# Cross attention's sample values computed in full fp32, with V standing still under columns of probabilities

## The chip, the cores and the metric

One Trainium2 chip, of which the program uses one core. The metric is the time of one execution on the device in microseconds (us), the median of several. Engines are named as in the profile: PE is TensorE's matmul, PEld its weight load, DVE is VectorE, ACT is ScalarE, POOL is GpSimd, SP is SyncE.

## The reference

One inference step of a two-layer decoder trunk, for a prompt of 256 tokens and for 8 sample sequences of one token each, in fp32. Each layer runs a feed-forward block, a mixer (state space and retention in layer 0, mLSTM in layer 1), cross attention and a second feed-forward block. The part that counts here is cross attention:

```python
def cross_attn(h, k, v, w_q, w_o):
    bsz, l, _ = h.shape
    q = (h @ w_q).reshape(bsz, l, X_HEADS, X_HEAD_DIM)
    s = jnp.einsum('blhd,bmhd->bhlm', q, k.astype(q.dtype)).astype(F32) * (X_HEAD_DIM ** -0.5)
    p = jax.nn.softmax(s, axis=-1).astype(h.dtype)
    o = jnp.einsum('bhlm,bmhd->blhd', p, v.astype(h.dtype)).reshape(bsz, l, D_MODEL)
    return o @ w_o
```

There are 4 heads of 256 dimensions over 256 memory tokens. The prompt's K and V are computed from `mem_prompt` by a linear layer (`w_xkv`) and are outputs too. Each of the 8 samples has K and V of its own, read from `cache_mem_k` and `cache_mem_v`: 256 x 1024 fp32 numbers, 1 MB each, for each sample and layer. For a sample, `o` is one row of probabilities for each head times that sample's V.

## The kernel before

The kernel is a list of stages. Each stage gives work to some of the five engines, and each engine runs its share of all stages in the order of the list; semaphores tie the engines together. So what stands ahead of a wait in an engine's list is done first, and what stands behind it waits too.

**Linear layers** (class `Linear`, L170) walk over chunks of 256 output columns. SP loads a chunk of weights (`raw`, four slots), ACT rounds it to its upper half (`whi`, L205), DVE subtracts to get the lower half (`wlo`, L211), two chunks ahead of PE. PE then does three products for each tile, upper by upper, upper by lower and lower by upper, so that two halves in the rounded type fp32r replace one fp32 product. A chunk is 2 output tiles x 8 k tiles x 3 products, which is 48 matmuls. A linear layer can have hooks: other stages, whose instructions are put behind the matmuls of chunk l on PE, and next to that chunk's step on the other engines.

**Cross attention** (function `cross`, L1653, run once for each layer) has two such linear layers over the memory: the K linear layer carries the samples' scores in its hooks (`SampleScores`, with `spread`, L708 and L709, which broadcasts a query row to all partitions), the V linear layer (L1873, `turned`, 256 columns, lines L247 to L249) carries the samples' values:

- hook 0: `SampleSoftmax`, and the transposes that bring the prompt's K into token order (`k_turn`);
- hook 1: `SplitV` for samples 0 and 1, `prob_turn` (two transposes that put the samples' probabilities into columns, `pTs`, memory tokens on partitions), `MaskProbs`, then `SampleValues` for samples 0 and 1;
- hooks 2 and 3: `SplitV` and `SampleValues` for samples 2 and 3, and 4 and 5;
- behind the layer: the same for 6 and 7, then `SampleRows`.

`MaskProbs` (L1781) spreads the probabilities over 64 columns with zeros between them, in two halves (`pmh`, `pml`), so that all samples can add into the same 8 rows of PSUM. `SplitV` (L1801) makes two halves of a sample's V: ACT writes `vh` (L1814), DVE writes `vl` over the loaded values (L1820). `SampleValues` (L1823) then needs, for each sample, 2 halves of the memory x 4 heads x 3 products = 24 matmuls (L1845 to L1847). The stationary operand is 128 x 8 (masked probabilities), and 256 columns of V stream. Each ends in rows (8 samples x 1024), which `SampleRows` copies out (L1853) and `SampleOut` transposes back into columns (L1860) while the prompt's scores run.

The loads of V go through POOL's queue in pieces of half a sample (`load_v`, L1684, 512 KB). `vc` holds two samples. The first four pieces are issued by `FirstV`, well ahead. Every later one waits until the matmuls on the piece two samples before it have ended (L1831), since `vl` is stored in place. `SampleValues`' loads are followed on POOL by the stores of the prompt's K and V (`Keep`, L1878).

Behind the stage come `Scores` (L1892, the prompt's scores; L1896 waits for all sample values), `SampleOut`, the transposes of the prompt's probabilities, `Values` (L1929, products at L1938), and the output projection.

In the profile, a matmul on fp32 operands shows as two records and one on fp32r as one: L2271 is 64 matmuls in the program and 128 records.

Of the kernel before, what the change touches and what calls it, by code (L numbers as in the profile page):

```python
# [14 lines left out]
F32 = mybir.dt.float32  # L15
F32R = mybir.dt.float32r
ALU = mybir.AluOpType
# [3 lines left out]
P = 128  # L21
D = 1024
KD = D // P
NP = 256
# [17 lines left out]
def build(nc, A, O):  # L42
    with ExitStack() as ctx:
# [755 lines left out]
        def mixer_ab():  # L799
# [819 lines left out]
            class RReady(Stage):  # L1619
                def pe(S, e):  # L1620
# [5 lines left out]
        X = {n: sem_of("x_" + n) for n in ("mem_in", "score", "nmax", "exp", "prob", "pv", "oh", "ol", "qb", "kused", "smax", "sexp", "sprob",  # L1626
                                           "spv", "soh", "sol", "qh", "ql", "vh", "vl", "pm", "pmh", "pml", "ost", "spo")}
        KR = 8
# [4 lines left out]
        def cross_buffers():  # L1633
# [9 lines left out]
                qtl=place("qtl", [NS, 2, 512], F32R, at=R + 82176), qth=place("qth", [NS, 2, 512], F32R, at=R + 88064),  # L1643
                ost=place("ost", [NS, 2, 512], at=R + 88064),
                vh=place("vh", [P, 2, 2, D], F32R, at=R + 65792), vl=place("vl", [P, 2, 2, D], F32R, at=R),
                pm=place("pm", [P, 8, 64], at=R + 92160), pml=place("pml", [P, 8, 64], F32R, at=R + 92160),
                pmh=place("pmh", [P, 8, 64], F32R, at=R + 94208),  sc=place("sc", [P, 2, 32], at=R + 86272),
                ps_=place("ps_", [32, MEM], at=R + 86528), pTs=place("pTs", [P, 64], at=R + 87552),
                st=place("st", [P, 4, 8], at=R + 87808), sst=place("sst", [32, 4], at=R + 87936),
                kc=[place(f"kc{i}", [P, 4, D], at=R + at) for i, at in enumerate((65792, 40960))],  # L1650
                 vc=place("vc", [P, 2, 2, D], at=R))

        def cross(layer):  # L1653
# [12 lines left out]
            class Load(Stage):  # L1666
# [8 lines left out]
                def dve(S, e):  # L1675
                    for q, n in kept:
                        e.wait_ge(q, n)
# [5 lines left out]

            def load_v(e, u):  # L1684
                e.dma_start(B.vc[:, u // 2 % 2, u % 2, :], A["cache_mem_v"][layer, u // 2, (u % 2) * P:(u % 2 + 1) * P].rearrange("p h d -> p (h d)")).then_inc(vc_in[u % 4], 16)

# [12 lines left out]
            class FirstV(Stage):  # L1699
                def pool(S, e):  # L1700
                    mem_split(e)
                    for u in range(4):
                        load_v(e, u)
            stages.append(FirstV())
# [75 lines left out]
            ps_ready = turned()  # L1780
            class MaskProbs(Stage):  # L1781


                def pool(S, e):
                    if lc:
                        e.wait_ge(X["sol"], lc)
                    e.memset(B.pm[:, :, :], 0.0).then_inc(X["pm"], 1)

                def dve(S, e):
                    ps_ready(e)  # L1790
                    e.wait_ge(X["pm"], 2 * lc + 1)
                    e.tensor_copy(B.pm[:, :, 0:64:9].rearrange("p (m h) b -> p m h b", m=2),
                                  B.pTs[:, :].rearrange("p (m b h) -> p m h b", m=2, b=NS)).then_inc(X["pm"], 1)
                    e.wait_ge(X["pmh"], lc + 1)
                    e.tensor_tensor(B.pml[:, :, :], B.pm[:, :, :], B.pmh[:, :, :].bitcast(F32), ALU.subtract).then_inc(X["pml"], 1)

                def act(S, e):
                    e.wait_ge(X["pm"], 2 * lc + 2)
                    nc.scalar.activation(B.pmh[:, :, :], B.pm[:, :, :], ACT.Copy).then_inc(X["pmh"], 1)

            class SplitV(Stage):  # L1801

                def __init__(S, b):
                    S.b = b

                def act(S, e):
                    b = S.b
                    if b < 2:
                        e.wait_ge(X["kused"], 2 * NS * (lc + 1))
                    for m_ in range(2):  # L1810
                        e.wait_ge(vc_in[2 * (b % 2) + m_], 16 * (4 * lc + b // 2 + 1))
                        if b >= 2:
                            e.wait_ge(X["spv"], 2 * (NS * lc + b - 2) + m_ + 1)
                        nc.scalar.activation(B.vh[:, b % 2, m_, :], B.vc[:, b % 2, m_, :], ACT.Copy).then_inc(X["vh"], 1)  # L1814

                def dve(S, e):
                    b = S.b
                    for m_ in range(2):
                        e.wait_ge(X["vh"], 2 * (NS * lc + b) + m_ + 1)
                        e.tensor_tensor(B.vl[:, b % 2, m_, :], B.vc[:, b % 2, m_, :], B.vh[:, b % 2, m_, :].bitcast(F32),  # L1820
                                        ALU.subtract).then_inc(X["vl"], 1)

            class SampleValues(Stage):  # L1823

                def __init__(S, b):
                    S.b = b

                def pool(S, e):
                    for u in (2 * S.b, 2 * S.b + 1):
                        if u + 4 < 2 * NS:  # L1830
                            e.wait_ge(X["spv"], 2 * NS * lc + u + 1)  # L1831
                            load_v(e, u + 4)

                def pe(S, e):
                    b = S.b
                    if b == 0:
                        e.wait_ge(X["pml"], lc + 1)
                    for m_ in range(2):
                        e.wait_ge(X["vl"], 2 * (NS * lc + b) + m_ + 1)
                        for h in range(XH):  # L1840
                            o = psum[0:NS, 4 + h // 2, (h % 2) * XD:(h % 2 + 1) * XD]
                            ph, pl = B.pmh[:, m_ * XH + h, b * 8:b * 8 + 8], B.pml[:, m_ * XH + h, b * 8:b * 8 + 8]
                            vh, vl = B.vh[:, b % 2, m_, h * XD:(h + 1) * XD], B.vl[:, b % 2, m_, h * XD:(h + 1) * XD]

                            e.matmul(o, ph, vh, start=b == 0 and m_ == 0 and h % 2 == 0, stop=False)  # L1845
                            e.matmul(o, ph, vl, start=False, stop=False)  # L1846
                            m = e.matmul(o, pl, vh, start=False, stop=b == NS - 1 and m_ == 1 and h % 2 == 1)  # L1847
                        m.then_inc(X["spv"], 1)

            class SampleRows(Stage):  # L1850
                def dve(S, e):
                    e.wait_ge(X["spv"], 2 * NS * (lc + 1))
                    e.tensor_copy(B.ost[:, :, :], psum[0:NS, 4:6, :]).then_inc(X["ost"], 1)  # L1853

            class SampleOut(Stage):

                def pe(S, e):
                    e.wait_ge(X["ost"], lc + 1)
                    for t in range(KD):
                        m = e.transpose(psum[:, 5, t * NS:(t + 1) * NS], B.ost[:, t // 4, (t % 4) * P:(t % 4 + 1) * P], ident[0:NS, 0:NS])  # L1860
                    m.then_inc(X["spo"], 1)

                def act(S, e):
                    e.wait_ge(X["spo"], lc + 1)
                    nc.scalar.activation(B.oh[:, :, NP:T], psum[:, 5, 0:64].rearrange("p (t b) -> p t b", t=KD), ACT.Copy).then_inc(X["soh"], 1)

                def dve(S, e):
                    e.wait_ge(X["soh"], lc + 1)
                    e.tensor_tensor(B.ol[:, :, NP:T], psum[:, 5, 0:64].rearrange("p (t b) -> p t b", t=KD), B.oh[:, :, NP:T].bitcast(F32),
                                    ALU.subtract).then_inc(X["sol"], 1)  # L1870

            SV, SP = [SampleValues(b) for b in range(NS)], [SplitV(b) for b in range(NS)]
            Linear(W, 4, KD, 2, by_cols(W, D), (B.mh, B.ml), dve=v_out, cols=256, turned=True, early=True,  # L1873
                   hooks={0: [SampleSoftmax()] + k_turn, 1: SP[0:2] + prob_turn + [MaskProbs()] + SV[0:2],
                          2: SP[2:4] + SV[2:4], 3: SP[4:6] + SV[4:6]})
            kv_out = evicted()
# [8 lines left out]
            stages.append(Keep())  # L1885
            for b in (6, 7):
                stages.extend([SP[b], SV[b]])
            stages.append(SampleRows())
            tot["stores"] += 32
            pending.append((stored["pool"], tot["stores"]))  # L1890

            class Scores(Stage):  # L1892

                def pe(S, e):
                    kv_out(e)
                    e.wait_ge(X["spv"], 2 * NS * (lc + 1))  # L1896
                    for u in range(8):
                        h, lb = u // 2, u % 2
                        if u >= 2:
                            e.wait_ge(X["exp"], 8 * lc + u - 1)  # L1900
                        for d in range(2):
                            m = e.matmul(psum[:, u % 2, 0:MEM], B.xq[:, 2 * h + d, lb * P:(lb + 1) * P], B.Kf[:, 2 * h + d, :], start=d == 0, stop=d == 1)  # L1902
                        m.then_inc(X["score"], 1)
# [519 lines left out]
```

## Time and profile before

| what | us |
|---|---|
| median of 3 runs | 2179.12 |
| lowest and highest | 2172.78, 2183.26 |
| the profiled execution | 2174.99 |
| its span, first to last instruction | 2173.2 |
| mean granted TensorE clock | 0.922 of 2.4 GHz |
| PE busy | 1906.6 (88%) |
| DVE busy | 1375.7 (63%) |
| ACT busy | 896.0 (41%) |

Three views serve here. The busy time by window cuts a stretch into pieces and gives for each how long an engine was busy, the records in it, and the clock that was granted to TensorE (1.00 is 2.4 GHz, 0.50 is 1.2 GHz). The waits say who waited for whom. The timeline lists instructions in order, with equal neighbours merged into one row: its start, its length from the first start to the last end, and the count of records.

### The profile page before, as it was taken

Reading aid. Unit: us, or ns where it says so; the run is one execution under the profiler, and the core shown is the slowest. Engines: PE = TensorE matmul, PEld = TensorE weight load, DVE = VectorE, ACT = ScalarE, POOL = GpSimd, SP = SyncE. Lnnn points to the kernel's source line nnn. Section 1 sums busy time; section 2 is a strip of 40 time slices with the busy share of each in tenths; the row PEclk is TensorE's granted clock in tenths of the full one; section 3 lists DMA queues with packets and bytes.
Section 4 is the critical chain, followed back from the end, with each engine's and each line's share of the span. In section 5 each row is a group of like instructions: output and inputs, shape, how many; then the busy total and the mean of one; then the engine's idle time right before and its main releaser. Section 6 shows DMA issues by size and latency. Waiting matters only on the chain. (4 is left out here: it accounts for less than half of the span.)

```text
span 2173.2 us, 35020 instructions
## 1 busy us (share of the span) xinstructions
PE 1906.6 (88%) x13769; PEld 1744.7 (80%) x13769; DVE 1375.7 (63%) x2352; ACT 896.0 (41%) x1143; POOL 202.1 (9%) x292
## 2 busy tenths in 40 slices
PE   6999886996688768998899999999968698899996
PEld 5999786985355467987779999999956597679996
DVE  4665595698767565448567656665652567557654
ACT  4434344346655445332434334433422532434331
POOL 0001101101111000111110011001001021110011
PEclk9999998899799888998999999999985898999998
DMA  6656852336778424666526656656606266526652
GB/s 179 181 163 188 156 168 65 113 117 189 247 261 298 148 79 114 176 233 232 203 90 182 184 160 191 186 157 195 191 29 163 78 217 229 206 86 174 185 160 82
DMA packets 462782, 361.49 MB, mean 166 GB/s; under 512 B 12297, under 2 KB 435493, under 8 KB 462629
## 3 DMA queue, kind: packets, MB, share of 16 engines
q1 hardware_dynamic: 409056, 254.35, 39.9%
q0 software_dynamic: 20192, 71.95, 10.8%
q10 hardware_dynamic: 33424, 33.70, 4.6%
q8 instruction: 72, 1.18, 0.2%
q14 instruction: 38, 0.31, 0.0%
HBM read 321.49 MB, written 38.66 MB: 166 GB/s over the span
## 5 line engine op out<-in xcount | busy, mean ns | idle before, releaser
L211 DVE TENSOR_TENSOR wlo<-raw,whi 128x2048 fp32r<-128x2048 f32 (+2 forms) x262 | 558.9, 2134 | 268.4 <-ACT whi L205 267.7
L252 PE MATMUL psum<-xnh,whi 128*128 128x264 f32 x2328 | 676.9, 291 | 10.1 <-DVE cols L885 9.8
L253 PE MATMUL psum<-xnl,whi 128*128 128x264 f32 x2328 | 668.7, 287 | 0.0
L254 PE MATMUL psum<-xnh,wlo 128*128 128x264 f32 x2328 | 667.5, 287 | 0.0
L205 ACT ACTIVATE whi<-raw 128x2048 fp32r<-128x2048 f32 (+2 forms) x262 | 463.3, 1770 | 190.7 <-DMA raw<-in_w_ffn_out 76.8
L252 PEld LDWEIGHTS psum<-xnh,whi 128*128 128x128 f32 x2328 | 449.0, 193 | 15.7 <-DVE cols L885 8.6
L253 PEld LDWEIGHTS psum<-xnl,whi 128*128 128x128 f32 x2328 | 448.8, 193 | 1.2
L254 PEld LDWEIGHTS psum<-xnh,wlo 128*128 128x128 f32 x2328 | 445.9, 192 | 0.0
L252 PE MATMUL psum<-Hh,whi 128*128 128x264 f32 x704 | 200.5, 285 | 0.0
L254 PE MATMUL psum<-Hh,wlo 128*128 128x264 f32 x704 | 200.0, 284 | 0.0
L253 PE MATMUL psum<-Hl,whi 128*128 128x264 f32 x704 | 199.1, 283 | 0.0
L722 ACT ACTIVATE sg<-sg 128x264 f32<-128x264 f32 x88 | 37.4, 425 | 288.0 <-DVE sg L726 287.9
L254 PEld LDWEIGHTS psum<-Hh,wlo 128*128 128x128 f32 x704 | 132.6, 188 | 0.0
L253 PEld LDWEIGHTS psum<-Hl,whi 128*128 128x128 f32 x704 | 132.5, 188 | 0.0
L252 PEld LDWEIGHTS psum<-Hh,whi 128*128 128x128 f32 x704 | 132.3, 188 | 0.0
L374 ACT ACTIVATE xnh<-x,g 128x264 fp32r<-128x264 f32 x56 | 27.6, 514 | 154.1 <-DVE x L384 83.8
L459 PE MATMUL psum<-sq,ones 128*128 128x264 f32 (+1 forms) x128 | 46.2, 504 | 43.3 <-ACT sq L445 42.4
L405 POOL TENSOR_TENSOR sq<-x 128x264 f32 (+1 forms) x52 | 39.5, 760 | 416.1 <-DVE x L382 217.1
L726 DVE TENSOR_TENSOR sg<-psum,rstd 128x264 f32<-128x264 f32 x88 | 38.0, 431 | 58.8 <-PE psum L254 58.7
L459 PEld LDWEIGHTS psum<-sq,ones 128*128 128x128 f32 x128 | 25.8, 236 | 58.8 <-issue 39.6
L393 POOL MEMSET acc<- 128x528 f32 x8 | 4.4, 544 | 735.3 <-DVE ht L729 533.0
L729 DVE TENSOR_TENSOR ht<-sg,psum 128x264 f32<-128x264 f32 x88 | 37.8, 430 | 54.4 <-ACT sg L722 54.4
(479 smaller groups left out, 3425.3 us busy)
## 6 DMA issues: line engine op xcount, KB each, us to landing
raw<-in_w_ffn_in SPq DMA_DIRECT2D x176, 512.0 KB, 4.9
raw<-in_w_in_ab SPq DMA_DIRECT2D x88, 512.0 KB, 4.4
raw<-in_w_ffn_out SPq DMA_DIRECT2D x64, 384.0 KB, 4.0
raw<-in_w_ffn_out SPq DMA_DIRECT2D x64, 320.0 KB, 3.3
sb<-in_state_ret POOLq DMA_DIRECT2D x32, 512.0 KB, 5.6
out<-sb ACTq DMA_DIRECT2D x32, 512.0 KB, 4.8
raw<-in_w_out_ab SPq DMA_DIRECT2D x32, 512.0 KB, 4.5
kc<-in_cache_mem_k POOLq DMA_DIRECT2D x32, 512.0 KB, 5.9
```

The costliest lines, as they stand in the source:

```text
L205: nc.scalar.activation(whi[:, c % SLOTS, 0:m], raw[:, c % SLOTS, 0:m], ACT.Copy).then_inc(hi_done, 1)
L211: nc.vector.tensor_tensor(wlo[:, c % SLOTS, 0:m], raw[:, c % SLOTS, 0:m], whi[:, c % SLOTS, 0:m].bitcast(F32), ALU.subtract).then_inc(lo_d ...
L252: e.matmul(out, a, hi[:, kk, 0:S.cols], start=first, stop=False)
L253: e.matmul(out, a, lo[:, kk, 0:S.cols], start=False, stop=False)
L254: m = e.matmul(out, b, hi[:, kk, 0:S.cols], start=False, stop=final)
L374: nc.scalar.activation(xnh[:, t, :], x[:, t, :], ACT.Copy, scale=g1[:, gcol + t:gcol + t + 1]).then_inc(xh_done, 1)
L393: e.memset(acc[:, :, :], 0.0).then_inc(acc_done, 1)
L405: e.tensor_tensor(sq[:, at, :], xs, xs, ALU.mult).then_inc(xs_ready, 1)
L459: e.matmul(psum[:, SSB, 0:S.n], ones[:, :], sq[:, t % 2, 0:S.n], start=t % S.g == 0, stop=t % S.g == S.g - 1).then_inc(ss_done, 1)
L722: nc.scalar.activation(sg[:, par, :], sg[:, par, :], ACT.Silu).then_inc(gate_ready, 1)
L726: e.tensor_tensor(sg[:, par, :], psum[:, 2 * par, 0:T], rstd1[:, 0, :], ALU.mult).then_inc(gate_scaled, 1)
L729: e.tensor_tensor(ht[:, par, :], sg[:, par, :], psum[:, 2 * par + 1, 0:T], ALU.mult).then_inc(bank_free, 1)
```

## The change

The samples' V is no longer split. `SampleValues` takes the loaded fp32 values as the stationary operand, a tile of 128 tokens x 128 dimensions, and streams one column: the probabilities of that sample and head, in fp32. For each sample there are 8 tiles of dimensions x 2 halves of the memory = 16 fp32 matmuls instead of 24 on fp32r, and each writes one column of PSUM, already in the layout that `SampleOut` wants. `MaskProbs`, `SplitV`, `SampleRows` and the 8 transposes of `SampleOut` go. `vc` becomes two tiles of two samples each; the second takes the place of half of the samples' K buffers, so `LaterV` loads samples 2 and 3 once the scores of sample 5 have been computed. Later loads wait for the matmuls of the sample four before, not two.

```diff
-                vh=place("vh", [P, 2, 2, D], F32R, at=R + 65792), vl=place("vl", [P, 2, 2, D], F32R, at=R),
-                 vc=place("vc", [P, 2, 2, D], at=R))
+                vc=[place(f"vc{i}", [P, 2, 2, D], at=R + at) for i, at in enumerate((0, 65792))])
...
-            def load_v(e, u):
-                e.dma_start(B.vc[:, u // 2 % 2, u % 2, :], A["cache_mem_v"][layer, u // 2, (u % 2) * P:(u % 2 + 1) * P].rearrange("p h d -> p (h d)")).then_inc(vc_in[u % 4], 16)
+            def load_v(e, b):
+                for m_ in range(2):
+                    e.dma_start(B.vc[b // 2 % 2][:, b % 2, m_, :],
+                                A["cache_mem_v"][layer, b, m_ * P:(m_ + 1) * P].rearrange("p h d -> p (h d)")).then_inc(vc_in[b % 4], 16)
...
+            class LaterV(Stage):
+                def pool(S, e):
+                    e.wait_ge(X["kused"], 2 * NS * lc + 12)
+                    for b in (2, 3):
+                        load_v(e, b)
...
             class SampleValues(Stage):
                 def pool(S, e):
-                    for u in (2 * S.b, 2 * S.b + 1):
-                        if u + 4 < 2 * NS:
-                            e.wait_ge(X["spv"], 2 * NS * lc + u + 1)
-                            load_v(e, u + 4)
+                    b = S.b
+                    if b + 4 < NS:
+                        e.wait_ge(X["spv"], NS * lc + b + 1)
+                        load_v(e, b + 4)
                 def pe(S, e):
                     b = S.b
                     if b == 0:
-                        e.wait_ge(X["pml"], lc + 1)
-                    for m_ in range(2):
-                        e.wait_ge(X["vl"], 2 * (NS * lc + b) + m_ + 1)
-                        for h in range(XH):
...
-                            e.matmul(o, ph, vh, start=b == 0 and m_ == 0 and h % 2 == 0, stop=False)
-                            e.matmul(o, ph, vl, start=False, stop=False)
-                            m = e.matmul(o, pl, vh, start=False, stop=b == NS - 1 and m_ == 1 and h % 2 == 1)
-                        m.then_inc(X["spv"], 1)
+                        ps_ready(e)
+                    e.wait_ge(vc_in[b % 4], 32 * (2 * lc + b // 4 + 1))
+                    for t in range(KD):
+                        h = t // 2
+                        for m_ in range(2):
+                            i = m_ * 32 + b * XH + h
+                            m = e.matmul(psum[:, 4, t * NS + b:t * NS + b + 1], B.vc[b // 2 % 2][:, b % 2, m_, t * P:(t + 1) * P], B.pTs[:, i:i + 1],
+                                         start=m_ == 0, stop=m_ == 1)
+                    m.then_inc(X["spv"], 1)
...
-            class SampleRows(Stage):
-                def dve(S, e):
-                    e.wait_ge(X["spv"], 2 * NS * (lc + 1))
-                    e.tensor_copy(B.ost[:, :, :], psum[0:NS, 4:6, :]).then_inc(X["ost"], 1)
...
             Linear(W, 4, KD, 2, by_cols(W, D), (B.mh, B.ml), dve=v_out, cols=256, turned=True, early=True,
-                   hooks={0: [SampleSoftmax()] + k_turn, 1: SP[0:2] + prob_turn + [MaskProbs()] + SV[0:2],
-                          2: SP[2:4] + SV[2:4], 3: SP[4:6] + SV[4:6]})
+                   hooks={0: [LaterV(), SampleSoftmax()] + k_turn, 1: prob_turn + SV[0:2], 2: SV[2:4], 3: SV[4:6]})
...
-            for b in (6, 7):
-                stages.extend([SP[b], SV[b]])
-            stages.append(SampleRows())
+            stages.extend(SV[6:8])
```

## Rows read from the trace of the kernel before

**Rows 1.** The page: the span and each engine's busy time.
```profile
span 2173.2 us, 35020 instructions
PE 1906.6 (88%) x13769; PEld 1744.7 (80%) x13769; DVE 1375.7 (63%) x2352; ACT 896.0 (41%) x1143; POOL 202.1 (9%) x292
```

**Rows 2.** Windows, PE alone, layer 0: stretch, length, busy (records), clock, DMA share, GB/s.
```profile
1046.30:1051.10 4.80, 0.31 (x3) 0.71 0.67 217
1051.10:1058.60 7.50, 7.49 (x49) 0.73 0.34 120
1058.60:1064.20 5.60, 5.60 (x50) 1.00 0.67 217
1080.90:1084.40 3.50, 0.00 (x0) 1.00 1.00 365
1084.40:1091.80 7.40, 7.26 (x48) 0.77 0.82 332
```

**Rows 3.** Waits, 1046 to 1092: engine, line, whom for: total, times, longest.
```profile
ACT vh L1814 <- DMA vc<-in_cache_mem_v: 21.4, 12, 5.7
PE psum L1845 <- DVE pml L1795: 4.5, 1, 4.5
PE psum L1845 <- DVE vl L1820: 3.7, 1, 3.7
```

**Rows 4.** Waits, the same stretch of layer 1, 1860 to 1906.
```profile
PE psum L1845 <- DVE pml L1795: 5.3, 1, 5.3
PE psum L1845 <- DVE vl L1820: 3.3, 1, 3.3
```

**Rows 5.** Chain that ended last, layer 1, before the last pair: start, us, what.
```profile
1892.01 4.65 DMA vc<-in_cache_mem_v
```

**Rows 6.** Timeline, ACT and DVE, layer 0: start, us, line, names, shapes, records.
```profile
1020.64 0.42 DVE L1739 CUSTOM_DVE_ANT_0 kc<-kc,psum 128x256 f32<-128x256 f32 x1
1046.64 0.22 ACT L616 ACTIVATE pTs<-psum 128x64 f32<-128x64 f32 x1 [0.19 <-PE psum L598]
```

**Rows 7.** The page's DMA issues: KB of each, us to landing.
```profile
vc<-in_cache_mem_v POOLq DMA_DIRECT2D x32, 512.0 KB, 5.8
```

**Rows 8.** Timeline, PE: a spread behind a K chunk; mLSTM's sample states (`SampleC`).
```profile
1004.85 0.50 PE L708 MATMUL psum<-qth,sel 8*128 8x512 f32 x1
...
1650.40 3.57 PE L2271 MATMUL psum<-cq,ccb 128*128 128x1 f32 x16
```

**Rows 9.** Timeline, PE, mLSTM's prompt states, layer 1.
```profile
1624.46 0.50 PE L2118 MATMUL psum<-ones,cktm 128*128 128x1 f32 x4
1625.77 0.39 PE L2118 MATMUL psum<-ones,cktm 128*128 128x1 f32 x3
```

**Rows 10.** Windows in `SampleC`: PE, PEld, DVE, ACT, POOL busy (records), clock, DMA.
```profile
1645.00:1650.00 5.00, 5.00 (x20) 4.53 (x20) 1.66 (x4) 3.55 (x9) 0.78 (x1) 0.50 0.68 229
```

**Rows 11.** Windows of 1 us, columns as in rows 10: K chunk, spreads, K chunk.
```profile
1006.00:1007.00 1.00, 1.00 (x6) 0.55 (x5) 0.92 (x5) 0.00 (x0) 0.00 (x0) 1.00 0.83 208
1007.00:1008.00 1.00, 1.00 (x7) 1.00 (x8) 1.00 (x7) 0.00 (x0) 0.17 (x1) 0.69 0.98 324
1017.00:1018.00 1.00, 1.00 (x10) 1.00 (x8) 1.00 (x7) 0.00 (x0) 0.00 (x0) 0.81 0.92 275
```

**Rows 12.** Windows of 1 us, columns as in rows 10: around the first pair.
```profile
1048.00:1049.00 1.00, 0.00 (x0) 0.00 (x0) 1.00 (x2) 0.00 (x0) 0.00 (x0) 0.67 1.00 344
1055.00:1056.00 1.00, 1.00 (x10) 0.71 (x9) 0.00 (x0) 0.00 (x0) 0.00 (x0) 0.91 0.58 164
```

**Rows 13.** Windows, PE alone, columns as in rows 2: a K chunk behind spreads.
```profile
1006.90:1014.30 7.40, 7.40 (x50) 0.77 1.00 336
```

**Rows 14.** Timeline, PE, end of the stage in layer 1.
```profile
1906.04 1.97 PE L1902 MATMUL psum<-Kf,xq 128*128 128x256 f32 x8
1915.35 0.66 PE L1860 MATMUL psum<-ident,ost 8*128 8x8 f32 x8
1917.36 1.06 PE L598 MATMUL psum<-ident,pp 128*128 128x128 f32 x8 [1.35 <-issue]
```

More of the change, by code:

```diff
@@ L1626, in build @@
         X = {n: sem_of("x_" + n) for n in ("mem_in", "score", "nmax", "exp", "prob", "pv", "oh", "ol", "qb", "kused", "smax", "sexp", "sprob",
-                                           "spv", "soh", "sol", "qh", "ql", "vh", "vl", "pm", "pmh", "pml", "ost", "spo")}
+                                           "spv", "soh", "sol", "qh", "ql")}
         KR = 8
@@ L1643, in cross_buffers @@
                 qtl=place("qtl", [NS, 2, 512], F32R, at=R + 82176), qth=place("qth", [NS, 2, 512], F32R, at=R + 88064),
-                ost=place("ost", [NS, 2, 512], at=R + 88064),
-                vh=place("vh", [P, 2, 2, D], F32R, at=R + 65792), vl=place("vl", [P, 2, 2, D], F32R, at=R),
-                pm=place("pm", [P, 8, 64], at=R + 92160), pml=place("pml", [P, 8, 64], F32R, at=R + 92160),
-                pmh=place("pmh", [P, 8, 64], F32R, at=R + 94208),  sc=place("sc", [P, 2, 32], at=R + 86272),
+                sc=place("sc", [P, 2, 32], at=R + 86272),
                 ps_=place("ps_", [32, MEM], at=R + 86528), pTs=place("pTs", [P, 64], at=R + 87552),
@@ L1701, in pool @@
                     mem_split(e)
-                    for u in range(4):
-                        load_v(e, u)
+                    for b in range(2):
+                        load_v(e, b)
             stages.append(FirstV())
@@ L1780, in cross @@
             ps_ready = turned()
-            class MaskProbs(Stage):
+            class LaterV(Stage):
                 def pool(S, e):
-                    if lc:
-                        e.wait_ge(X["sol"], lc)
-                    e.memset(B.pm[:, :, :], 0.0).then_inc(X["pm"], 1)
-                def dve(S, e):
[L1790 to L1809, printed above, removed]
-                    for m_ in range(2):
[L1811 to L1821, printed above, removed]
+                    e.wait_ge(X["kused"], 2 * NS * lc + 12)
+                    for b in (2, 3):
+                        load_v(e, b)
             class SampleValues(Stage):
@@ L1836, in pe @@
                     if b == 0:
-                        e.wait_ge(X["pml"], lc + 1)
-                    for m_ in range(2):
-                        e.wait_ge(X["vl"], 2 * (NS * lc + b) + m_ + 1)
-                        for h in range(XH):
-                            o = psum[0:NS, 4 + h // 2, (h % 2) * XD:(h % 2 + 1) * XD]
-                            ph, pl = B.pmh[:, m_ * XH + h, b * 8:b * 8 + 8], B.pml[:, m_ * XH + h, b * 8:b * 8 + 8]
-                            vh, vl = B.vh[:, b % 2, m_, h * XD:(h + 1) * XD], B.vl[:, b % 2, m_, h * XD:(h + 1) * XD]
-                            e.matmul(o, ph, vh, start=b == 0 and m_ == 0 and h % 2 == 0, stop=False)
-                            e.matmul(o, ph, vl, start=False, stop=False)
-                            m = e.matmul(o, pl, vh, start=False, stop=b == NS - 1 and m_ == 1 and h % 2 == 1)
-                        m.then_inc(X["spv"], 1)
@@ L1850, in cross @@
-            class SampleRows(Stage):
-                def dve(S, e):
-                    e.wait_ge(X["spv"], 2 * NS * (lc + 1))
-                    e.tensor_copy(B.ost[:, :, :], psum[0:NS, 4:6, :]).then_inc(X["ost"], 1)
-            class SampleOut(Stage):
[L1857 to L1861, printed above, removed]
+                        ps_ready(e)
@@ L1863, in act @@
+            class SampleOut(Stage):
                 def act(S, e):
-                    e.wait_ge(X["spo"], lc + 1)
-                    nc.scalar.activation(B.oh[:, :, NP:T], psum[:, 5, 0:64].rearrange("p (t b) -> p t b", t=KD), ACT.Copy).then_inc(X["soh"], 1)
+                    e.wait_ge(X["spv"], NS * (lc + 1))
+                    nc.scalar.activation(B.oh[:, :, NP:T], psum[:, 4, 0:64].rearrange("p (t b) -> p t b", t=KD), ACT.Copy).then_inc(X["soh"], 1)
                 def dve(S, e):
                     e.wait_ge(X["soh"], lc + 1)
-                    e.tensor_tensor(B.ol[:, :, NP:T], psum[:, 5, 0:64].rearrange("p (t b) -> p t b", t=KD), B.oh[:, :, NP:T].bitcast(F32),
+                    e.tensor_tensor(B.ol[:, :, NP:T], psum[:, 4, 0:64].rearrange("p (t b) -> p t b", t=KD), B.oh[:, :, NP:T].bitcast(F32),
@@ L1870, in dve @@
                                     ALU.subtract).then_inc(X["sol"], 1)
-            SV, SP = [SampleValues(b) for b in range(NS)], [SplitV(b) for b in range(NS)]
+            SV = [SampleValues(b) for b in range(NS)]
             Linear(W, 4, KD, 2, by_cols(W, D), (B.mh, B.ml), dve=v_out, cols=256, turned=True, early=True,
-                   hooks={0: [SampleSoftmax()] + k_turn, 1: SP[0:2] + prob_turn + [MaskProbs()] + SV[0:2],
-                          2: SP[2:4] + SV[2:4], 3: SP[4:6] + SV[4:6]})
+                   hooks={0: [LaterV(), SampleSoftmax()] + k_turn, 1: prob_turn + SV[0:2], 2: SV[2:4], 3: SV[4:6]})
@@ L1895, in pe @@
                     kv_out(e)
-                    e.wait_ge(X["spv"], 2 * NS * (lc + 1))
+                    e.wait_ge(X["spv"], NS * (lc + 1))
                     for u in range(8):
```

## Prediction

> **What bounds the kernel now.** I read the page first: PE is busy 88% of the span, the next engine 63% [rows 1]. So most stages end when PE ends. Then the windows on the stage that changes: between `prob_turn` and the prompt's scores, PE waits 4.5 us, does a pair of samples in 7.5, a V chunk in 5.6, a pair, a chunk, a pair, waits 3.7 and does the last pair in 7.3 [rows 2, 3]. The other two pairs run at clock 1.00 like the chunk and last 5.6 each. From 1046.6, the end of `prob_turn`, to 1091.9, the first of the prompt's scores, that is 45.3 us. Layer 1 has the same pieces with waits of 5.3 and 3.3, and I take 45.9 [rows 4]. The sum of both stages is 91 us, 4% of the span, and on PE nothing hides them.
>
> The reader is to see two things. The first wait ends last with `pml`, at the end of a row of work on ACT and DVE (four splits, mask, halves). The second ends with `vl`: in the chain of layer 1 a transfer of 4.65 us, issued only when the matmuls freed the buffer, stands before the last split [rows 5]. And the pairs that PE enters after a wait are slow since the clock is at 0.50: they take 7.5 and 7.3 us instead of 5.6.
>
> **What goes, part by part.** The first wait: PE now needs only the copy of `pTs`, which takes 0.22 us on ACT right after the transposes [rows 6]; I take 0.35 with the semaphores. The copy is DVE's in layer 1, and the splits ahead of it are gone. Gain 4.5 - 0.35 = 4.15 in layer 0 and 4.95 in layer 1.
>
> The second wait: samples 4 and 5 reload the buffer of 0 and 1, whose matmuls end a chunk, a pair and another chunk before they are wanted, over 20 us; 6 and 7 likewise. Two pieces need 5.8 us each from issue to landing and overlap [rows 7]. So the gain is the whole 3.7 and 3.3 us. What is late next is nothing: samples 2 and 3 wait on POOL for the scores of sample 5, read by 1021 [rows 6], 40 us before their use. Queued behind this new wait on POOL are only the later V loads, `Keep`'s stores and a memset, all due later. The stores no longer meet V loads.
>
> The splits (16 of 1.06 us on ACT and 1.24 on DVE for each layer), the masks, the copy in `SampleRows` and the transposes give nothing beyond those waits: ACT and DVE have room, and the 0.66 us of transposes stand ahead of 1.35 us in which PE waits for the prompt's probabilities [rows 14]. I cost them at nothing; without that cover they would be worth 0.7 us a layer.
>
> **What comes.** 16 fp32 matmuls for each sample are 32 records, against 24. `SampleC` in mLSTM does the very same operation: fp32 tile of 128x128 standing, one column moving. 16 records take 3.57 us, of which the last one's 0.35 is not pitch: 3.22/15 = **0.215 us a record at clock 0.50** [rows 8, 10]. At clock 1.00 the nearest is L2118, the same shapes: three records take 0.39 and four 0.50, so **0.11 us** [rows 9], half, as it should be if the loading of weights follows the clock. So a pair of samples (64 records) costs 7.0 us at 1.00 and 13.8 at 0.50; before it was 5.6 and, all at 0.50, 10.2.
>
> **Which clock?** This decides. In `SampleC`, windows show PE busy 5.00 of 5.00 us and the clock at 0.50 [rows 10]; the seven windows of 5 us behind it in that stage say the same, 40 us in all. Its work is these matmuls and four spreads of 8 rows. It never raised the clock. That such work also loses a clock that is high shows in the K layer: behind a dense chunk the spreads begin at 1004.85, PE stays busy 1.00 of 1.00, and the clock falls at about 1007.4 (0.69 over 1007 to 1008), 2.5 us later; the next time the chunk ends at 1014.3 and it falls at 1017.6, 3.3 later [rows 8, 11, 13]. When PE idles from 1046.6 it falls at 1048.3, 1.7 later [rows 12]. So I take it that a pair begins at 1.00 and falls after 2.5 us (bounds 1.7 and 3.3).
>
> - Pair 1 starts 0.35 after `prob_turn`, so 2.15 us at 1.00 are 20 records, and 44 x 0.215 = 9.5: 11.7.
> - Pairs 2 and 3, each behind a chunk that has brought the clock back: 2.5 us for 23 records, 41 x 0.215 = 8.8: 11.3 each.
> - Pair 4 stands right behind pair 3: all at 0.50, 13.8.
> - The two chunks between start at 0.50. The first pair of before, which is dense too, took until 1055.1 to get the clock back, 4.0 us from its start [rows 12], and lost 1.9 us; a K chunk behind spreads lasts 7.4 instead of 5.6 [rows 13]. I take 7.5.
> - The prompt's scores start at 0.50 too. Eight records take 1.97 us at 1.00 [rows 14] and up to twice that; with 4 us at half clock and the waits for ACT between them I take 1.5 (bounds 0 and 3).
>
> Sum for layer 0: 0.35 + 11.7 + 7.5 + 11.3 + 7.5 + 11.3 + 13.8 = 63.5, against 45.3: +18.2, with the scores +19.7. Layer 1: 63.4 against 45.9, +17.5, with the scores +19.0. Together +38.7. The profiled execution took 2174.99 us (span 2173.2 and 1.8 around it), so it would take 2213.7. The median of the runs is 4 us above it; I forecast **2215**.
>
> **Rivals.** *A: the clock holds.* PE has no gap any more in this stage, and records fill it. If weights being loaded count as work, the clock stays at 1.00. Then the stage is 0.35 + 4 x 7.0 + 2 x 5.7 = 39.8, less than 45.3 and 45.9 by 5.5 and 6.1: 2174.99 - 11.6 = 2163, and 2167 against the median. The point from which it decides: going from 1.00 to 0.50 adds 27 us to the 256 records of a layer, so the change gains as long as less than a fifth of them (5.5 of 27) run at 0.50. For it: every fall of the clock in this stage before came after idle time. Against it: rows 10, where the same loads fill PE and the clock stays down. They show only that a low clock isn't raised, not that a high one is lost; rows 11 show that for spreads of 8 rows, not for these. So I leave it 0.12.
>
> The Trainium skill ("TensorE: Matmul & The Clock Gate", section "Why this matters for your kernels") says that gaps in which PE idles between bursts bring the clock down, and asks for none; by that rule this kernel would end at A's time. The windows of the K layer speak against reading it so, since PE was busy 1.00 of 1.00 us as the clock fell. The same page (section "LDWEIGHTS (loading the stationary operand)") gives a load as columns over 1.2 GHz, at either clock: an estimate of 107 ns a record, hence 27 us for the 256 records of a layer, again A's time. The rows agree at clock 1.00 (0.11) and not at 0.50 (0.215).
>
> *B: the clock doesn't come back in the chunks.* A chunk wholly at 0.50 costs 48 x 0.213 = 10.2 us. Then each layer has 4 x 13.8 + 2 x 10.2 = 75.6, +30 and with the scores +33: 2241. Against it: it came back within 4.0 us in the first pair of before. 0.05.
>
> *C: the clock falls only in the last two pairs,* or late in each, since the chunks between feed it. Falls in half the places: +10 a layer, 2190 to 2198. 0.07. *D: a new wait for V.* If the loads for samples 2 and 3 met the linear layer's weights in the K stage, PE would wait some us for a chunk, on top of the forecast; they have 40 us. It stays in the forecast's range.
>
> **How the numbers follow.** Forecast 0.76, A 0.12, B 0.05, C 0.07. The forecast's own range: falls after 3.3 us instead of 2.5 take 0.8 x 3 off each layer, chunks at 6.8 take 1.4, no cost in the scores 1.5: -5.3 a layer, 2204. With falls after 1.7 (+2.4), chunks at 8.5 (+2.0) and scores at 3 (+1.5) it is +5.9 a layer, 2227. With the 4 us by which single runs lie on either side, and C's upper part, I give **2197 to 2231**; A, B and C's rest are left out. About 0.5% (11 us) is what a measurement of this kernel can tell from no change: slower than 2190 in forecast, B and most of C, 0.87; A lies at the edge of half a per cent, 0.06 within and 0.06 faster; 0.01 of C within.
>
> **What would show it.** Right: no wait ahead of the first and of the last pair; 256 records a layer, 128*128 with one column, 0.11 us apart at first and then 0.215; clock 0.50 in most windows of the pairs, in all of pair 4; the two chunks at 7 to 8 us; `SampleC`, the feed-forward blocks and the K layer as before. Wrong: windows at 1.00 within the pairs (A); waits of PE for V or for weights; a pitch other than in rows 8 and 9, for instance if two records of one matmul share more than in L2271.

## The result, and the profile after

The kernel after takes **2215.2 us** (median of four runs, 2214.1 to 2222.8), where the one before took 2178.3 beside it (four runs): a ratio of 1.018, with a 95% interval of 1.014 to 1.021. The forecast was 2215. The profiled execution of after is its slowest, 2222.8 us, 7.6 above the median; so I read pieces of stages from it, and its total is looked at by itself further down.

The page of after: the span, the engines' busy time, the chain that ended last by lines, and the new group, whose columns are busy time and mean ns of one, then the idle time before.

```profile
span 2220.6 us, 35140 instructions
PE 1967.7 (89%) x13881; PEld 1813.7 (82%) x13881; DVE 1334.7 (60%) x2314; ACT 862.0 (39%) x1109; POOL 201.2 (9%) x290
...
PE psum L252 17%; PE psum L253 17%; PE psum L254 17%; PE psum L1809 4%; ACT whi L205 3%; PE psum L598 2%; PE psum L459 2%; DVE wlo L211 1%; PE psum L2220 1%; DMA raw<-in_w_in_ab 1%; DVE sl L1546 1%; PE psum L708 1%; PE psum L1568 1%; DVE hb L1315 1%; PE psum L709 1%
...
L1809 PE MATMUL psum<-pTs,vc 128*128 128x1 f32 x512 | 90.7, 314 | 0.7 <-issue 0.4
```

PE is busy for 61 us more than in [rows 1], DVE 41 us less and ACT 34 us less: the work on the halves went, and PE's busy time grew. The new line L1809 (the fp32 records, `psum<-pTs,vc`) holds 4% of the chain alone, nearly all of its 90.7 us. The waits that changed, from 1052 to 1116 in layer 0 (engine, line, whom for: total, times, longest):

```profile
POOL vc L1683 <- PE psum L1809: 50.4, 4, 29.1
PE psum L1809 <- ACT pTs L616: 0.3, 1, 0.3
```

Of PE's two waits of 4.5 and 3.7 us [rows 3] 0.3 is left. POOL stands up to 29.1 us before the V loads of the later samples, until the matmuls have read the buffer. It did so in before too (62.3 us in 12 waits, up to 41.1), and in after PE shows no wait for V: the loads land in time.

Windows with PE alone, layer 0, columns as in [rows 2]: the end of `prob_turn`, pair 1, chunk, pair 2, chunk, pairs 3 and 4.

```profile
1052.40:1053.05 0.65, 0.35 (x3) 1.00 0.00 0
1053.05:1065.45 12.40, 12.39 (x64) 0.56 0.49 170
1065.45:1073.90 8.45, 8.45 (x49) 0.64 0.35 125
1073.90:1083.35 9.45, 9.45 (x66) 0.74 0.67 224
1083.35:1091.40 8.05, 8.05 (x49) 0.67 0.36 130
1091.40:1115.20 23.80, 23.70 (x130) 0.58 0.36 133
```

The reader is to see that from pair 1 on length and busy time are nearly the same in every row: PE has no gap, and yet these rows have a clock between 0.56 and 0.74. Pair 2 of before, which [rows 2] do not show, ran at clock 1.00:

```profile
1064.20:1069.60 5.40, 5.40 (x50) 1.00 0.78 268
```

It took 5.4 us; here pairs 1 and 2 take 12.4 and 9.5. And the chunks, in which nothing was changed, take 8.45 and 8.05 instead of 5.6. Layer 1 has the same pieces: pair 1, chunk, pair 2, chunk, pairs 3 and 4:

```profile
1894.00:1904.40 10.40, 10.40 (x64) 0.67 0.58 203
1904.40:1911.65 7.25, 7.25 (x49) 0.77 0.40 145
1911.65:1922.45 10.80, 10.80 (x66) 0.64 0.56 196
1922.45:1930.80 8.35, 8.35 (x50) 0.65 0.34 126
1930.80:1954.30 23.50, 23.39 (x130) 0.59 0.36 135
```

Windows of 1 us, columns as in [rows 10], show a fall within pair 1, and one within pair 3:

```profile
1053.00:1054.00 1.00, 0.94 (x9) 0.94 (x9) 0.24 (x1) 1.00 (x2) 0.00 (x0) 1.00 0.31 59
1054.00:1055.00 1.00, 1.00 (x9) 1.00 (x9) 0.16 (x1) 0.81 (x1) 0.00 (x0) 0.73 0.96 329
1055.00:1056.00 1.00, 1.00 (x6) 1.00 (x6) 1.00 (x1) 0.00 (x0) 0.00 (x0) 0.50 1.10 388
...
1094.00:1095.00 1.00, 1.00 (x11) 1.00 (x10) 0.00 (x0) 0.00 (x0) 0.92 (x2) 1.00 1.19 372
1095.00:1096.00 1.00, 1.00 (x9) 1.00 (x8) 0.00 (x0) 0.00 (x0) 0.00 (x0) 0.71 0.93 302
1096.00:1097.00 1.00, 1.00 (x6) 1.00 (x7) 0.00 (x0) 0.00 (x0) 0.00 (x0) 0.50 1.05 410
```

PE and PEld are busy for the whole microsecond in which the clock goes from 1.00 (2.4 GHz) to 0.50 (1.2 GHz). Ahead of pair 1 stands a wait of 0.31 us; ahead of the fall in pair 3 PE had been busy without a gap since that wait, for some 42 us. The Trainium skill ("TensorE: Matmul & The Clock Gate", section "Why this matters for your kernels") puts the loss of the clock down to gaps in which PE idles; this trace disagrees, with 1.00 of 1.00 us busy.

At 0.50, a stretch of the timeline in pairs 3 and 4 (start, us, line, names, shapes, records) gives the pitch: (11.45 - 0.35)/52 = 0.213 us a record.

```profile
1103.65 11.45 PE L1809 MATMUL psum<-pTs,vc 128*128 128x1 f32 x53
```

**Where the difference of the profiled spans lies.** After minus before is 47.4 us. From the end of `prob_turn` to the prompt's scores layer 0 takes 62.5 instead of 45.3 us (+17.2), layer 1 60.7 instead of 45.9 (+14.8). The scores take 1.7 us longer in each. Of the rest, 6.1 us had arisen before the first such stage, 8.5 arise between the two stages, and 2.5 are given back in layer 1 behind the scores (12.5 us for transposes and values instead of 15.1); after that both need 240.8. The stages and scores, 35.4 us, come near the 36.9 by which the medians differ. The other 12 are not shown to come from the change. After's profiled execution lies 7.6 above its median, and these stretches differ between the traces of the other kernels too. The first stage begins (end of `prob_turn`) at 1039.4 us in cols64 and at 1052.8 in after. The stretch between the stages takes 767.3 us in after, 768.3 in cols64 and 767.2 in dense24. In mlstm112, which has before's cross attention and an edit worth 12.3 us in this stretch, it takes 754.3, which would be 766.6 without the edit. So it is the trace of before, with 758.9, that is short there; what makes it so is open. (cols64, dense24 and mlstm112 are experiments of the next section.)

### The profile page after: what moved, and what is told of

It reads as the page before. It is cut to its first block, busy times and chain, and to the rows that moved or that the text cites. A ratio compares the mean times of both kernels' runs of the same rounds, so it can differ in the third digit from the quotient of the medians.

```text
span 2220.6 us, 35140 instructions
## 1 busy us (share of the span) xinstructions
PE 1967.7 (89%) x13881; PEld 1813.7 (82%) x13881; DVE 1334.7 (60%) x2314; ACT 862.0 (39%) x1109; POOL 201.2 (9%) x290
## 4 chain that ended last, share of the span: by engine, by line
PE 72%; DVE 11%; ACT 7%; issue 6%; DMA 3%; SPq 0%; POOL 0%; ACTq 0%; DVEq 0%; POOLq 0%
PE psum L252 17%; PE psum L253 17%; PE psum L254 17%; PE psum L1809 4%; ACT whi L205 3%; PE psum L598 2%; PE psum L459 2%; DVE wlo L211 1%; PE psum L2220 1%; DMA raw<-in_w_in_ab 1%; DVE sl L1546 1%; PE psum L708 1%; PE psum L1568 1%; DVE hb L1315 1%; PE psum L709 1%
## 5 line engine op out<-in xcount | busy, mean ns | idle before, releaser
L1809 PEld LDWEIGHTS psum<-pTs,vc 128*128 128x128 f32 x512 | 90.7, 281 | 0.9 <-issue 0.4
L1809 PE MATMUL psum<-pTs,vc 128*128 128x1 f32 x512 | 90.7, 314 | 0.7 <-issue 0.4
```

What stands on the lines that cost most here:

```text
L1809: m = e.matmul(psum[:, 4, t * NS + b:t * NS + b + 1], B.vc[b // 2 % 2][:, b % 2, m_, t * P:(t + 1) * P], B.pTs[:, i:i + 1], start=m_ == 0, ...
```

## The experiments

**The theory:** the clock falls since each record streams one column only (I call such work thin, and work with 256 columns a record dense); the loading of 128 columns of weights for each does not keep it up. **The first rival:** something else in the new stage costs it: the pattern of loads, the fp32 records themselves, transfers that run beside them, or the row of pieces. **The second:** the clock is not all; the waits that went were worth little, or V comes late.

### 64, 16, 112 and 32 columns instead of one (cols64, cols16, cols112, cols32)

The column of probabilities is broadcast, so that each matmul streams it several times over; the results go to neighbouring columns of psum, and each later product overwrites the columns that the one before wrote beyond its own. The copy behind them reads the new layout. Number, order and size of the weight loads, the matmuls, the DMAs and the waits are the same.

```diff
-  m = e.matmul(psum[:, 4, t * NS + b:t * NS + b + 1],
-               B.vc[b // 2 % 2][:, b % 2, m_, t * P:(t + 1) * P], B.pTs[:, i:i + 1],
+  m = e.matmul(psum[:, 4, b * KD + t:b * KD + t + 64],
+               B.vc[b // 2 % 2][:, b % 2, m_, t * P:(t + 1) * P],
+               B.pTs[:, i:i + 1].to_broadcast([P, 64]),
...
-  psum[:, 4, 0:64].rearrange("p (t b) -> p t b", t=KD)
+  psum[:, 4, 0:64].rearrange("p (b t) -> p t b", t=KD)
```

> The changed kernel, with the one column of probabilities streamed 64 times over (a broadcast read; 64 equal columns are written and the next product overwrites 63 of them). Same 512 records, same weight loads, same transfers. Theory (the clock is the cost): the stream keeps the clock at 1.00, records stand 0.11 us apart, a pair of samples takes 7.0 us, the stage some 40 us instead of 62, and the whole is near 2178 - 11 = 2167, faster than before. Rival (the loads of fp32 weights are slow in such a stream whatever the clock): nothing changes, 2215. Rival (64 columns don't hide behind the load): each record is up to 0.05 us longer, 2167 + 27 = 2194.

Measured: **2169.3 us** (ten runs), 0.997 of before (0.9948 to 0.9992), 46 us less than after, and 44.6 less than cols16, which was measured beside it. Windows of layer 0, PE alone, the same pieces as above:

```profile
1039.10:1039.70 0.60, 0.31 (x3) 1.00 0.00 0
1039.70:1046.90 7.20, 7.17 (x65) 1.00 0.68 230
1046.90:1052.60 5.70, 5.70 (x51) 1.00 0.72 264
1052.60:1059.65 7.05, 7.05 (x67) 1.00 0.72 214
1059.65:1065.30 5.65, 5.65 (x50) 1.00 0.78 292
1065.30:1079.85 14.55, 14.43 (x130) 1.00 0.59 217
```

The clock is 1.00 in every window, the pairs last 7.2 us and less, the chunks 5.7, as before the change (5.6). The stage is 40.5 us in both layers; rival A of the prediction had put it at 39.8. The group of L1809 by form (busy time, mean ns of one, idle before):

```profile
L1809 PE MATMUL psum<-pTs,vc 128*128 128x64 f32 x512 | 58.0, 275 | 0.7 <-issue 0.4 <-ACT pTs L616 0.3
```

The 512 records take 58.0 us instead of 90.7, that is 0.113 each: 64 times the columns, and less time. The stages account for it: 62.5 + 60.7 - 2 x 40.5 = 42.2, and 2 x 1.7 in the scores, 45.6 of the 46 us. The program's transfers, waits and loads are the same, so none of them brought the clock down by itself: with 64 columns instead of one it stayed up.

> As cols64, with 16 columns. Theory: so short a stream doesn't hold the clock, the records are 0.215 us apart for most of each pair, 2215 as the changed kernel. If the clock hung on whether PE had gaps at all, or on the count of instructions, then cols16 and cols64 would both be like the changed kernel.

Measured: 2213.8 us (four runs), 1.018 (1.015 to 1.021), no different from after.

```profile
1047.45:1056.80 9.35, 9.33 (x65) 0.76 0.64 225
1056.80:1065.10 8.30, 8.30 (x50) 0.65 0.38 129
1065.10:1074.70 9.60, 9.60 (x67) 0.72 0.66 218
1074.70:1082.60 7.90, 7.90 (x49) 0.69 0.36 133
1082.60:1106.55 23.95, 23.84 (x130) 0.58 0.36 132
```

These are the pieces of after without the end of `prob_turn`: the clock falls in pairs 1, 2 and 3, and the chunks get it back. The stages take 59.4 and 60.6 us (after: 62.5 and 60.7). So the broadcast itself or the other layout of psum gives nothing to speak of, and with 16 columns the clock fell as with one.

> As cols64, with 112 columns. Theory: the clock holds as well, and comes back within the pairs where it was lost before; if the stream still hides behind the load of 128 columns the time is that of cols64, 2165; if not, records are longer than 0.11 us and the time lies above cols64 by up to 512 x 0.04 = 20 us.

Measured: 2168.0 us (ten runs), 0.9973 (0.9954 to 0.9992), the same as with 64. The group by form:

```profile
L1809 PE MATMUL psum<-pTs,vc 128*128 128x112 f32 x512 | 58.2, 275 | 0.7 <-issue 0.4 <-ACT pTs L616 0.3
```

And the window of pairs 3 and 4, layer 0, PE alone:

```profile
1070.55:1085.15 14.60, 14.46 (x130) 1.00 0.59 217
```

58.2 us for 512 records with 112 columns and 58.0 with 64: the streaming lies behind the load of the next weights. While the clock holds, more columns give no more.

> As cols64, with 32 columns: between 16, where the clock fell as with one, and 64, where it never fell. Theory: a time between 2169 and 2214, depending on how often it falls; no change of the spacing of records at either clock (0.11 and 0.215).

Measured: 2207.7 us in the one run. The window of pairs 3 and 4:

```profile
1078.05:1102.00 23.95, 23.86 (x130) 0.58 0.36 132
```

It is 23.95 us again, at 0.58, and the stage of layer 0 takes the 59.4 us of cols16. So the clock fell with 32 columns and not with 64. Layer 1 takes 57.6 us instead of 60.6; that and the total, some us under the 2213.8 of 16 columns, are one run and no finding.

**What these runs do not separate.** They change the columns while all 128 rows of the array are fed. The K layer's spreads stream 512 columns each, but through 8 rows, and the clock fell just behind them as well: they run from 1004.85 to 1006.9, and it fell at about 1007.4, with PE busy throughout [rows 8, 11]. That suggests that a long stream alone does not keep the clock. Whether the columns count, or rows and columns together, is open.

### The dense values of before, without the waits (dense24)

What are the waits worth that the change removed? This kernel keeps after's buffers and loads, and puts back the masks, the 24 records a sample, each streaming 256 columns, `SampleRows` and the transposes. The splits of V stay out: the matmuls stream another fp32r buffer in the place of V's halves, so V's part in the result is left out.

```diff
+            class MaskProbs(Stage):
...
-                        ps_ready(e)
+                        e.wait_ge(X["pml"], lc + 1)
-                            m = e.matmul(psum[:, 4, t * NS + b:t * NS + b + 1], ...
+                            vh = B.mh[:, m_ * XH + h, :]
+                            e.matmul(o, ph, vh, start=b == 0 and m_ == 0 and h % 2 == 0, stop=False)
+                            e.matmul(o, ph, vh, start=False, stop=False)
+                            m = e.matmul(o, pl, vh, start=False, stop=b == NS - 1 and m_ == 1 and h % 2 == 1)
```

> The changed kernel's buffers, loads and waits, but the kernel before's masks and 24 streams of 256 columns for each sample, read from the memory's upper half that lies in the same memory instead of V (V is left out of the result; nothing is split). It takes the removed waits alone. Theory: the first wait shrinks from 4.5 and 5.3 us to about 2.3 (copy, mask, two halves), the second goes, all pairs take 5.6: some 8 us less in each layer, 2178 - 17 = 2161. Rival (the waits return somewhere else, at a transfer or at the next linear layer): no change, 2178.

Measured: 2155.9 us (four runs), 0.991 (0.988 to 0.994): 19 us under the 2174.9 of before beside it. Of PE's waits in layer 0 one is left, for the masked halves (total, times, longest):

```profile
PE psum L1833 <- DVE pml L1796: 2.0, 1, 2.0
```

Windows of layer 0, PE alone: that wait, pair 1, chunk, and pairs 3 and 4:

```profile
1047.40:1049.65 2.25, 0.30 (x3) 0.95 0.48 122
1049.65:1056.60 6.95, 6.94 (x48) 0.77 0.46 156
1056.60:1062.20 5.60, 5.60 (x50) 1.00 0.85 322
...
1073.30:1084.45 11.15, 11.05 (x98) 1.00 0.77 284
```

The stage is 36.8 us in layer 0 and 35.5 in layer 1, 18.9 less than before in the sum, which is the 19 of the medians. The waits give 12.8 of it: 16.8 us of before [rows 3, 4], less the 2.0 that are left in each layer. The other 6.1 are in the main what the waits had cost behind them, the clock: the last pair took 7.4 us at 0.77 in [rows 2], and here two pairs take 11.15 at 1.00. Pair 1 is still slow, 6.95 us at 0.77, behind the wait that is left; the expectation had put all pairs at 5.6. So taking away the splits and waits of V was worth 19 us; after gave that up and 37 more. Its records, beside dense ones, cost 59 us (2215.2 - 2155.9). Of these, 46 are the clock (cols64 against after). The other 13 are in part the loads: a pair of 64 records costs 7.2 us at clock 1.00 and one of 48 costs 5.6, 12.8 us for eight pairs, less the 4.0 that dense24 still waits for the masks; that is 8.8, and the stages differ by 8.7 (81.0 against 72.3). What is left, some 4 us, lies within the intervals of the two medians.

### The same records in mLSTM (mlstm112)

`SampleC` in layer 1 holds the same operation in both kernels, and it stood at 0.50 all along [rows 10]. If columns are what counts, 112 of them must raise a low clock there too. The edit on the kernel before:

```diff
-  t = (2 * h + i) * NS + b
-  m = e.matmul(psum[:, 3, t:t + 1], cb[:, b % 4, h, i * P:(i + 1) * P],
-               q[:, h, NP + b:NP + b + 1], start=True, stop=True)
+  t = b * 8 + 2 * h + i
+  m = e.matmul(psum[:, 3, t:t + 112], cb[:, b % 4, h, i * P:(i + 1) * P],
+               q[:, h, NP + b:NP + b + 1].to_broadcast([P, 112]), start=True, stop=True)
```

> The kernel before with that edit at mLSTM's sample products alone; cross attention is untouched. Theory: 14 us less than before, 2175 - 14 = 2161. Rival: 2175.

Measured: 2161.7 us (seven runs), 0.993 (0.9905 to 0.996), 17 us under before. Windows, PE alone, samples 1 to 4 of eight:

```profile
1645.75:1651.40 5.65, 5.65 (x20) 0.50 0.65 220
1651.40:1657.10 5.70, 5.70 (x21) 0.50 0.62 184
1657.10:1661.95 4.85, 4.85 (x22) 0.61 0.71 216
1661.95:1665.00 3.05, 3.05 (x21) 1.00 0.66 172
```

The records of the second and the fourth in the timeline:

```profile
1651.43 3.75 PE L2271 MATMUL psum<-cq,ccb 128*128 128x112 f32 x16
...
1661.94 2.04 PE L2271 MATMUL psum<-cq,ccb 128*128 128x112 f32 x16
```

The clock comes back at 1660.9, at the end of the third, and a sample then takes 3.05 us instead of 5.65. `SampleC` is 30.0 us long instead of 39.9, and the linear layer behind it, which no longer starts at 0.50, 5.9 instead of 8.3: 12.3 of the 17 us. Of the other 5, 4.2 are the distance of before's median (2179.2) from the execution that its profile shows (2175.0). The two traces differ elsewhere too (the stretch between the stages of cross attention, in which `SampleC` lies, is only 4.5 us shorter), so the 17 rests on the medians and the 12.3 on the stage. That the records at 0.50 take 3.75 us instead of 3.57 is the price of the 112 columns there. The loads are the ones that stood at 0.50 before: with 112 columns beside them the clock came back.

### Both edits: a version that beats both kernels (both112, both144)

> cols64, and the same broadcast with 112 columns at mLSTM's sample products (L2271 of the kernel before, the very rows from which the forecast took its 0.215 us). Theory (the columns streamed decide the clock): the clock comes back to 1.00 inside that stage, its records go from 0.215 to 0.11 us and the spreads to half, so a sample takes 2.8 us of PE instead of 5.5; loads and stores of the states then set the pace at some 4 us, the stage loses about 12 us, and the linear layer behind it starts at 1.00 (2 more). 2169 - 14 = 2155. Rival (that stage is bound by its transfers or by VectorE): 2169, no change against cols64.

This is after with 64 columns in cross attention and 112 in mLSTM. Measured: **2154.0 us** (six runs, 2149.1 to 2165.6), 0.989 (0.986 to 0.9915) of before, 61 us less than after. Its profiled execution is the slowest of the six, 2165.6 us, and `SampleC` takes 39.7 us in it against 30.0 in mlstm112: the clock comes back late. Windows, PE alone, of sample 6 and of samples 7 and 8:

```profile
1673.50:1679.20 5.70, 5.70 (x21) 0.50 0.27 92
1679.20:1684.80 5.60, 5.60 (x33) 0.62 0.27 94
```

Here the clock came back only at 1683.5, in the last sample, with the instructions of mlstm112 in this stage. So this profile does not show the gain of the mLSTM half. That the five faster runs have it is likely, since 9.7 us would account for most of the 11.6 between this run and the median, but they have no trace. To see the mechanism and to try whether a wider stream raises the clock more surely, the columns in mLSTM were made 144:

> both112 with 144 columns at mLSTM's sample products (64 in cross attention as before). In the profile of both112 the clock stayed at 0.50 for most of that stage and in that of mlstm112 it came back at the fourth sample. Theory: with a longer stream it comes back earlier, at the first or second sample, and the times spread less; records are at most 0.12 us at 1.00, so the median is that of both112 or up to 5 us less, 2149 to 2154. Rival: the stream no longer hides behind the load and the gain is eaten, 2156 or more.

Measured: 2155.2 us (four runs, 2150.5 to 2156.2), 0.990 (0.987 to 0.993): no different from 112 columns, and between what the theory (up to 2154) and the rival (from 2156) had expected, so the time decides for neither. Windows, PE alone: the records of sample 1, its spreads, then sample 2 with its own:

```profile
1643.70:1647.85 4.15, 4.14 (x17) 0.50 0.74 255
1647.85:1649.00 1.15, 1.15 (x5) 0.95 0.26 86
1649.00:1652.30 3.30, 3.30 (x21) 1.00 0.63 167
```

The records of the two samples in the timeline:

```profile
1643.71 4.21 PE L2220 MATMUL psum<-cq,ccb 128*128 128x144 f32 x16 [8.74 <-DVE ccb L2231]
...
1649.01 2.25 PE L2220 MATMUL psum<-cq,ccb 128*128 128x144 f32 x16
```

The clock is back behind the first sample, and `SampleC` takes 25.8 us instead of 39.9. The price is in the last row: 2.25 us for 16 records instead of 2.04 with 112 columns. The expectation that a record takes at most 0.12 us was too low: the records stand 0.13 us apart at 1.00. What the earlier clock gives, some 4 us (25.8 against 30.0 in mlstm112), lies within the scatter of the runs. Whether 144 columns raise it in each execution, I can't say from one trace.

## Why the prediction was right

**What bounds, what goes.** PE had no other work in the stage, and what the stages and scores lost, 35.4 us, is nearly the 36.9 of the medians. The first wait became 0.31 us (taken: 0.35), the second 0. Nothing was late in its place: V's loads had the time. The forecast counted the waits that go as 4.15, 3.7, 4.95 and 3.3, 16.1 us; dense24 shows 19 with 4 us of waiting left, since the waits had cost clock behind them as well. In after this part came to nothing, because every pair loses its clock in any case, and the forecast had priced the pairs of both kernels with their clocks.

**The pitch.** 0.11 us at clock 1.00 and 0.215 at 0.50 were read from L2118 and `SampleC` [rows 8, 9]; in after's own records 0.110 and 0.213 were measured. That another stage held the very same operation in shape and type is what made this term firm.

**The clock.** It fell, and for the reason that rows 10 held ready: one column a load keeps PE busy and the clock low. Rival A's reason, loads that count as work, is refuted: cols64 and after load the same weights, and only their columns differ. Its time, on the other hand, was right for a kernel that holds the clock: 2167 worked out, 2169 and 2168 measured with 64 and 112 columns. B did not come: each chunk brought the clock back. C came in small part: the clock fell in pairs 1, 2 and 3 of both layers and was low all through pair 4, but four of the six falls came 3.6 us or more after the pair's start, later than the forecast's bound of 3.3. D left no trace: PE's waits in the K layer are the same before and after (4.8, 4.7 and 0.3 us in layer 0).

**The sizes, term by term** (us, taken, then layers 0 and 1; stretches start to start):

| term | taken | layer 0 | layer 1 |
|---|---|---|---|
| wait | 0.35 | 0.31 | 0.36 |
| from the pair's start to the fall (pairs 1, 2, 3) | 2.15, 2.5, 2.5 | 1.4, 4.4, 4.0 | 3.6, 3.0, 4.3 |
| pair 1 | 11.7 | 12.4 | 10.4 |
| pair 2 | 11.3 | 9.5 | 10.8 |
| pairs 3 and 4 | 25.1 | 23.8 | 23.5 |
| two chunks | 15.0 | 16.5 | 15.6 |
| scores, added | 1.5 | 1.7 | 1.7 |
| sum of the stage | 63.5, 63.4 | 62.5 | 60.7 |

The clock held for 9.8 and 10.8 us of the pairs instead of 7.15, worth 2.4 and 3.4 us in the pairs, since a microsecond at 1.00 does the work of two. The step that was mis-sized is thus the time to the fall: the K layer's spreads gave 2.5 and 3.3 us, and I took the lower. The values here range from 1.4 to 4.4, beyond both bounds, and one fixed value is a simplification. The chunks went the other way by 1.5 and 0.6 us: three of four took over 8 us. The chunks and scores give back 2.5 of the pairs' 5.8 us, so the terms of the sum missed by 3.3 (38.7 against 35.4).

That the forecast of 2215 was met to a fraction of a microsecond is luck. The sum gave 2213.7 from the profiled execution and, with the 4 us to the median, 2217.8; I put 2215 between them without a working. On the median of before as it came out, 2178.3, the sum gives 2217.0, and 2215.2 was measured.

**What would show it.** No wait ahead of the first and last pair, 512 records of 128*128 with one column, the pitches, the clock at 0.50 all through pair 4: all there. The chunks, expected at 7 to 8 us, took 7.25 to 8.45, three of the four over 8. `SampleC` as before: yes, at 0.50 in every window of after too.

## What to carry to other kernels

Standing the large operand still and moving one column saves matmuls and preparation, but here it took the clock from 2.4 to 1.2 GHz, for itself and for dense work behind it; look for such an operation elsewhere in the profile, with its granted clock, before you count loads. If the weight load sets the pitch anyway, try streaming the same column 64 times or more: it cost next to nothing beside the load and was worth 46 us here. The pattern was found, and with 112 columns was worth 17 us, in a stage that the change had not touched. Read the clock beside the busy share: PE was busy 1.00 of the time at either speed.

## What the runs showed of the hardware

- PE lost the clock while it was busy all the time, with an fp32 load of 128 columns under each record: with 1, 16 and 32 streamed columns it fell, with 64 and 112 it stayed at 1.00 through a stage of 40 us. It fell too behind spreads of 512 columns through 8 rows [rows 8, 11].
- Streaming 64 or 112 columns cost next to nothing beside an fp32 weight load at clock 1.00 (58.0 and 58.2 us for 512 records; the records stand 0.111 and 0.112 us apart, with one column 0.110). At 0.50 there was a price (3.75 instead of 3.57 us for 16), and with 144 columns at both levels (2.25 instead of 2.04 at 1.00).
- A dense chunk of 5.6 us took 7.25 to 8.45 behind thin work, without a wait.
- The time at which a low clock came back in mLSTM was not the same for the same instructions around it: with 112 columns at the end of the third sample in one kernel (mlstm112, 1660.9) and only at the end of the stage in the other (both112, 1683.5). What decides it is open.
